# Modulation rows by a table per slot, low halves one tile later, output's first tiles in two parts, context three steps later

## The chip, the cores and the metric

One core of a Trainium2 chip runs one program. The metric is the device time of one execution in microseconds (us). Engines are called PE (matmuls), PEld (weight loads, beside PE), DVE, ACT, POOL and SP (which issues most DMAs).

## The reference, cut to what matters

x is 512 positions by 1024 features. Two blocks run one after the other.

```
first_block, for l in 0, 1:
  mod = (silu(c) @ ada_w[l] + ada_b[l])            # 9 vectors of 1024
  h += 0.5 * mod[0,2] * swiglu(modulated norm of h, ffn_w_in[l,0], ffn_w_out[l,0])
  z = (modulated norm of h) @ mix_w_in[l]          # q, kv, gates, uv, za, zb
  y_a = sparse attention (compressed keys, all blocks, window), 8 heads of 64
  u, v = split(gelu(z_uv)); y_b = u * (causal W_s @ layernorm(v) + b)   # gated unit
  merged = sigmoid(za) * (y_a @ proj_a) + sigmoid(zb) * (y_b @ proj_b)
  h += mod[1,2] * (merged @ w_out[l])
  h += 0.5 * mod[2,2] * swiglu(modulated norm of h, ffn_w_in[l,1], ffn_w_out[l,1])
x = rmsnorm(h)
second_block: pool mixer and squared-relu MLP on latents (512) and context (256), then
  attention over both and a last MLP, modulated by w_ada_2 (for c_2, and partly for c_ctx_2)
```

## The kernel before, in words

**Products.** Every float32 operand of a large product is split into a high half (rounded, type fp32r) and a low half (the remainder), and a product is three matmuls: high x high, high x low, low x high (lines 584 to 586). For weights ACT writes the high half WH (L476) and DVE the low half WL (L489) of each tile of up to 128x2048; for activations likewise (names in H and L, as hH/hL, mH/mL, ybH/ybL, nHc/nLc).

**Slots.** `plan()` lists the 308 weight tiles, called slots, in the order in which PE uses them. There are 2 raw buffers and 4 of WH and WL (NR, NW = 2, 4). Each engine's program is written out by hand and walks the slots: `step_act`, `step_dve` and `step_pool` stand where PE begins slot k; they split the weights of slot k+3, whose buffers are free once slot k-1 is done. SP loads `raw(k+5)` at its turn k, after waiting for the low half of slot k+3.

**Modulation rows.** The vectors mod are computed on DVE: 240 "rows", each a 128x1024 tile of modulation weights times the broadcast condition, summed along the tile (`rows_dve`, L550). `rows_after(k)` says how many rows are done by slot k: one per slot, with pauses. Rows 0 to 143 and 208 to 239 take one such instruction. Rows 144 to 207 serve two conditions and take two 128x512 instructions (L559), a small sum (L563) and the one of L550. Rows from 15 on go through two buffers `araw`. SP's turn k loads, behind `raw(k+5)`, the rows up to one beyond `rows_after(k)`: so of the rows of slot k the first has been loaded a turn earlier, and a second one is issued at turn k, after DVE has done the low half of slot k+3. At slot 128 (`CHANGE`) SP replaces the condition, behind row 143. The steps at entries of a stage (`enter_dve`) do one row more.

**The mixer.** A stage is entered in halves of 256 positions: `both_halves_pe` runs the last product of the stage before (`network_end_pe` or `output_end_pe`, 8 output tiles for each half), while DVE updates h (L1196) and makes the norm. Then `attention1_pe` begins with two slots of key and value columns; ACT copies the first results to `cm`, DVE builds the blocks R from them (L1595, L1599), PE multiplies them (L1378). The attention itself has no slots. After it `gmlp_pe` computes u and v, four tiles "sv" (L1771) in two free PSUM banks, since four are set aside, and DVE makes of each tile: sum with the bias (L1821, which frees the bank), product with u (L1826), wait for ACT's high half (L1793), low half (L1828). `merged_act` and `merged_dve` apply the sigmoids through one scratch tile `scr[0]`. The output product (`output_end_pe`) takes each of 8 tiles through all 8 feature tiles mH/mL in turn; tiles 6 and 7 come last from the merge.

**The last gated network and the context.** In the network of layer 1 that follows the mixer (slots 159 to 195) the second block's context runs beside it: `weave(main, side, pace)` does one step of the network, then `pace(n)` steps of the context, on all four engines alike. `beside_network(n)` is 0 for n = 0, then 1, and 2 where n % 3 == 1. The context's steps: 1 to 3 sums of squares (DVE L661), 4 the sum on PE (L619, its root on ACT, L646), 5 its spread over partitions (L626, which needs DVE's L672), pool slots (w_pool_2) at steps 12, 17, 22 and 27, each needing low halves (L2052) that DVE makes a step earlier, a second norm with the sum at step 31 and the spread at 32, a third at 39 and 40. POOL_CONTEXT places the pool slots in `plan()`. The slots of the context's MLP (196 to 231) have no rows.

Of the kernel before, what the change touches and what calls it, by code (L numbers as in the profile page):

```python
# [6 lines left out]
F32 = mybir.dt.float32  # L7
# [8 lines left out]
S = 512  # L16
# [10 lines left out]
POOL_CONTEXT = (11, 15, 18, 22)  # L27
# [70 lines left out]
CHANGE = 8 * 18 - 16  # L98
# [242 lines left out]
def build(nc, A, out):  # L341
# [3 lines left out]
    with ctx:  # L345
# [159 lines left out]

        def rows_after(k):

            idle = max(0, min(k, SHARED[1] - 1) - SHARED[0] + 1)
            late = min(2, max(0, k - CHANGE + 1))
            return min(8 * len(adas), 17 + k - idle - late)  # L510
# [718 lines left out]
        def output_end_pe(g):  # L1229

            k0 = now.pe
            now.pe += 4

            def group(pe, x, o):
                k, c = k0 + o // 2, lat.half[x].cols
                b, free = take(g, "O", x, o)
                pe.wait_ge(*a_whi.to(k))
                pe.wait_ge(*wlo(k))
                products(pe, k, o % 2, KT, b[:, 0:S // 2], lambda i: (M.mH[:, i, c], M.mL[:, i, c]),
                         lambda i: (a_hhi.to(g, "m", i), v_hlo.to(g, "m", i)), (g, "O", x, o), free)  # L1240
                if x and o % 2:
                    mm.again("slot", k)
            return group
# [13 lines left out]
        def enter_act(act, l, j):  # L1257
            prev, g = stage_before(l, j), f"mix{l}" if j == 1 else f"ffn{l}{j // 2}"
            k0 = now.act
            now.act += 4 if j == 2 else 3  # L1260
            split_act(act, k0 + NW)
            rows_act(act, rows_after(k0) + 1)
            both_halves_act(act, g, mod(1, l, 3 * j), lambda x, i: v_h.to(prev, "O", x, i),
                            output_ahead(k0) if j == 2 else network_ahead(k0))

        def enter_dve(dve, l, j):
# [4 lines left out]
            rows_dve(dve, rows_after(k0) + 1)  # L1271
# [523 lines left out]
        def gmlp_dve(dve, g, l):  # L1795
# [22 lines left out]
            for f in range(4):  # L1818
                v = M.vf[:, f, :].rearrange("p (a b) -> p a b", a=4)
                dve.wait_ge(*mm.to(g, "sv", f))  # L1820
                dve.q.tensor_tensor(v, bank(g, "sv", f)[:, :].rearrange("p (a b) -> p a b", a=4),  # L1821
                                    M.bsb[:, f, :].unsqueeze(1).broadcast_to([128, 4, 128]), ALU.add
                                    ).then_inc(*empties(v_ev, g, "sv", f))
                dve.wait_ge(*v_ev.to(g, "sv", f))
                dve.wait_ge(*a_ev.to(g, "uv", f))
                dve.q.tensor_tensor(M.vf[:, f, :], M.vf[:, f, :], M.uu[:, f, :], ALU.mult).then_inc(*v_ev.up(g, "uv", f))  # L1826
                dve.wait_ge(*a_yhi.to(g, "yb", f))
                dve.q.tensor_tensor(M.ybL[:, f, :], M.vf[:, f, :], M.ybH[:, f, :].bitcast(F32), ALU.subtract  # L1828
                                    ).then_inc(*v_ylo.up(g, "yb", f))
# [14 lines left out]
        def merged_act(act, g):  # L1844
            sg = lat.scr[0]
            before = None
            for m in range(4):
                for which in range(2):
# [3 lines left out]
                    for f in (2 * m, 2 * m + 1):  # L1852
                        act.wait_ge(*mm.to(g, "z", which, f))
                        if before is not None:
                            act.wait_ge(*v_mg.to(*before))
                        act.q.activation(sg[:, :], bank(g, "z", which, f)[:, :], ACT.Sigmoid
                                         ).then_inc(*empties(a_fn, g, "z", which, f))
                        before = (g, "sum", f) if which else (g, "p", 0, f)
# [5 lines left out]
        def merged_dve(dve, g):  # L1864
            sg = lat.scr[0]
            for m in range(4):
                for which in range(2):
# [3 lines left out]
                    for f in (2 * m, 2 * m + 1):  # L1871
                        y = lat.scr[1 + f % 2]
# [691 lines left out]
        def beside_network(n):  # L2564
            return 0 if n < 1 else 1 + (n % 3 == 1)
# [66 lines left out]
        def sp_program(sp):  # L2632
# [33 lines left out]
            loaded = 16  # L2666
            for k in range(len(slots)):
                if k == CHANGE:
# [136 lines left out]
```

## Time and profile before

| what | value |
|---|---|
| median of 3 runs | 3920.36 us (3917.42 to 3921.22) |
| the profiled execution's own time | 3915.16 us |
| its span | 3913.4 us |
| mean granted clock of PE, as a share | 0.962 |
| PE busy | 3668.9 us (94%) |
| DVE, ACT, POOL busy | 2231.8, 1311.4, 341.8 us |

The span runs from the first to the last instruction of the program; the remaining 1.8 us lie around it. In the timeline, the brackets behind an instruction give how long its engine was idle before it and who ended that. In the listing of stretches the granted clock is a share of full speed, 0.50 being the lower of the two levels.

### The profile page before, as it was taken

How to read it: one execution, taken by the hardware profiler on the slowest of the kernel's cores; microseconds unless marked ns; L12 is line 12 of the kernel's file. 1: busy time of each engine (PE TensorE's matmuls, PEld its weight loads, DVE VectorE, ACT ScalarE, POOL GpSimd, SP SyncE). 2: the span in 40 equal slices, each digit the busy share in tenths (PEclk: the TensorE clock that was granted, in tenths of full speed). 3: DMA queues.
4: the chain of work that ended last, by engine and by line, in shares of the span. 5: the costliest groups of instructions: out<-in, count | busy, mean ns of one | idle time of the engine just before them, and what ended most of it. 6: DMA issues, size and time to landing. Idle time of an engine off the chain costs nothing.

```text
span 3913.4 us, 45537 instructions
## 1 busy us (share of the span) xinstructions
PE 3668.9 (94%) x18026; PEld 2962.2 (76%) x18026; DVE 2231.8 (57%) x3607; ACT 1311.4 (34%) x1906; POOL 341.8 (9%) x380
## 2 busy tenths in 40 slices
PE   6999899999999999999999999887799969999997
PEld 5888856788889888855788878777588846577886
DVE  5554644656446545554666767776755555634444
ACT  3222443233223222444224323344322234533221
POOL 0000122000001000112001010134100010200000
PEclk9999999999999999989999999998899968999998
DMA  5433301334432433310343434333233311012221
GB/s 225 167 145 145 120 33 59 127 137 164 146 145 102 183 139 144 126 69 25 124 162 124 149 143 161 124 119 140 87 145 145 135 49 54 1 44 85 89 97 42
DMA packets 84228, 451.93 MB, mean 115 GB/s; under 512 B 10193, under 2 KB 10641, under 8 KB 47153
## 3 DMA queue, kind: packets, MB, share of 16 engines
q1 hardware_dynamic: 81936, 439.35, 30.5%
q0 software_dynamic: 2080, 9.67, 0.7%
q8 instruction: 144, 2.36, 0.2%
q14 instruction: 68, 0.55, 0.0%
HBM read 446.88 MB, written 2.10 MB: 115 GB/s over the span
## 4 chain that ended last, share of the span: by engine, by line
PE 80%; DVE 9%; issue 4%; ACT 4%; DMA 1%; POOL 1%; SPq 0%; DVEq 0%; POOLq 0%; ACTq 0%
PE ps L584 21%; PE ps L586 21%; PE ps L585 21%; PE ps L1453 3%; PE ps L1489 2%; ACT WH L476 1%; DVE WL L489 1%; DVE scrc L1115 1%; PE ps L2418 1%; PE ps L1471 1%; DMA araw<-in_ast 1%; DVE scr L661 1%; PE ps L2392 1%; PE ps L958 1%; PE ps L604 1%
## 5 line engine op out<-in xcount | busy, mean ns | idle before, releaser
L584 PE MATMUL ps<-nH,WH 128*128 128x512 f32 x2416 | 956.9, 396 | 9.2 <-DVE nL L716 7.1
L489 DVE TENSOR_TENSOR WL<-raw,WH 128x2048 fp32r<-128x2048 f32 (+2 forms) x290 | 639.2, 2208 | 555.8 <-ACT WH L476 554.7
L586 PE MATMUL ps<-nH,WL 128*128 128x512 f32 x2416 | 953.1, 395 | 0.0
L585 PE MATMUL ps<-nL,WH 128*128 128x512 f32 x2416 | 951.0, 394 | 0.0
L476 ACT ACTIVATE WH<-raw 128x2048 fp32r<-128x2048 f32 (+2 forms) x308 | 560.0, 1823 | 583.8 <-PE ps L586 554.4
L584 PEld LDWEIGHTS ps<-nH,WH 128*128 128x128 f32 x2416 | 457.7, 189 | 118.7 <-issue 10.4
L585 PEld LDWEIGHTS ps<-nL,WH 128*128 128x128 f32 x2416 | 457.6, 189 | 103.5 <-issue 2.2
L586 PEld LDWEIGHTS ps<-nH,WL 128*128 128x128 f32 x2416 | 457.3, 189 | 99.4
L584 PE MATMUL ps<-hH,WH 128*128 128x512 f32 x1072 | 422.2, 394 | 2.2 <-DVE h L1185 2.2
L586 PE MATMUL ps<-hH,WL 128*128 128x512 f32 x1072 | 421.8, 393 | 0.0
L585 PE MATMUL ps<-hL,WH 128*128 128x512 f32 x1072 | 421.5, 393 | 0.0
L550 DVE SCALAR_TENSOR_TENSOR araw<-araw,cB 128x1024 f32<-128x1024 f32 x225 | 276.5, 1229 | 73.3 <-DMA araw<-in_ast 73.2
L1068 ACT ACTIVATE hH<-scr 128x512 fp32r<-128x512 f32 x152 | 96.1, 632 | 456.7 <-DVE scr L1112 382.9
L584 PEld LDWEIGHTS ps<-hH,WH 128*128 128x128 f32 x1072 | 201.4, 188 | 48.5 <-DVE h L1185 2.7
L585 PEld LDWEIGHTS ps<-hL,WH 128*128 128x128 f32 x1072 | 201.4, 188 | 46.2
L586 PEld LDWEIGHTS ps<-hH,WL 128*128 128x128 f32 x1072 | 201.4, 188 | 46.2
L1061 ACT ACTIVATE scr<-ps 128x512 f32<-128x512 f32 x152 | 89.5, 595 | 387.5 <-PE ps L586 379.2
L931 POOL TENSOR_SCALAR scr<-scr,der,mods 128x256 f32<-128x256 f32 x80 | 61.8, 773 | 1532.9 <-DVE scr L844 1532.0
L1118 DVE TENSOR_TENSOR hL<-scr,hH 128x512 fp32r<-128x512 f32 x152 | 105.3, 692 | 106.1 <-ACT hH L1068 106.1
L1185 DVE SCALAR_TENSOR_TENSOR h<-ps,der,h 128x512 f32<-128x512 f32 x144 | 102.6, 747 | 66.9 <-PE ps L586 65.4
L2108 DVE TENSOR_TENSOR ma<-ma,ps 128x512 f32<-128x512 f32 x112 | 74.7, 684 | 111.6 <-PE ps L586 111.2
L1664 DVE TENSOR_REDUCE st<-ps 128x1 f32<-128x128 f32 (+3 forms) x128 | 62.0, 486 | 111.1 <-PE ps L1455 111.0
(357 smaller groups left out, 5432.6 us busy)
## 6 DMA issues: line engine op xcount, KB each, us to landing
raw<-in_wst SPq DMA_DIRECT2D x282, 1024.0 KB, 4.8
araw<-in_ast SPq DMA_DIRECT2D x225, 512.0 KB, 5.7
raw<-in_wst SPq DMA_DIRECT2D x18, 512.0 KB, 3.6
row<-in_ast SPq DMA_DIRECT2D x15, 512.0 KB, 15.0
cw<-in_cw POOLq DMA_DIRECT2D x4, 1024.0 KB, 6.0
h<-in_xT SPq DMA_DIRECT2D x1, 2048.0 KB, 8.3
raw<-in_wst SPq DMA_DIRECT2D x8, 256.0 KB, 2.6
out<-h SPq DMA_DIRECT2D x8, 256.0 KB, 2.0
```

The lines of the kernel that those rows point to most:

```text
L476: act.q.activation(M.WH[k % NW][:, 0:n], M.raw[k % NR][:, 0:n], ACT.Copy).then_inc(*a_whi.up(k))
L489: dve.q.tensor_tensor(M.WL[k % NW][:, 0:n], M.raw[k % NR][:, 0:n], M.WH[k % NW][:, 0:n].bitcast(F32), ALU.subtract).then_inc(*v_wlo.up(k))
L550: dve.q.scalar_tensor_tensor(out=w[:, :], in0=w[:, :], scalar=1.0, in1=M.cB[q][:, :], op0=ALU.mult, op1=ALU.mult, accum_out=total).then_in ...
L584: pe.q.matmul(to, hi[:, i, cc], xh, start=i == 0, stop=False)
L585: pe.q.matmul(to, hi[:, i, cc], xl, start=False, stop=False)
L586: t = pe.q.matmul(to, lo[:, i, cc], xh, start=False, stop=i == nk - 1)
L1061: act.q.activation(p.scr[n % 2][:, 0:N], bank(g, "a", ci, f)[:, 0:N], ACT.Silu if gated else ACT.Relu).then_inc(*empties(a_fn, g, "a", ci, f))
L1068: act.q.activation(hH[:, ci % 2, f, :], p.scr[2 + f % 2][:, 0:N], ACT.Copy).then_inc(*a_hhi.up(g, ci, f))
L1118: dve.q.tensor_tensor(hL[:, ci % 2, f, :], p.scr[2 + u][:, 0:N], hH[:, ci % 2, f, :].bitcast(F32), ALU.subtract).then_inc(*v_hlo.up(g, ci, f))
L1185: dve.q.scalar_tensor_tensor(out=M.h[:, o, :], in0=bank(g, "o", ci, o)[:, :], scalar=gate[:, o:o + 1], in1=M.h[:, o, :], op0=ALU.mult, op1 ...
L1453: pe.q.matmul(b[:, 0:nk], M.q[half, hh // 2, 128 * qt:128 * qt + 128], K[half, 0:nk], start=True, stop=False, skip_group_check=True)
L1489: t = pe.q.matmul(to[half, 128 * x:512], M.Vt[br - 1][:, x, 64 * grp:64 * grp + 64], M.PT[br - 1][:, x, 128 * x:512], start=br == 1 and x ...
```

## The change

It has five parts.

1. `row_steps` makes a table `row_plan`: 1 row per slot, 2 at every third slot (k % 3 == 0) whose array's name begins with f (the gated networks), 0 at the last three output slots of each gated network but the last, at the mixer's first six slots, at proj_a, proj_b and w_out, and at the slots 196 to 231 as before. The row extra at entries is gone. The swap of the condition comes at slot 123 where the table holds still at 144 for two slots.
2. `gmlp_dve`: the low half of a tile comes after the sum and product of the next tile.
3. `merged_act`, `merged_dve`: two scratch tiles (scr[0], scr[3]) for the sigmoids in turn.
4. `output_end_pe`: the first four tiles of the first half are taken through feature tiles 0 to 5, and then all four through 6 and 7.
5. `beside_network(n)` is 0 for n < 4, then 1, and 2 where n is even; POOL_CONTEXT moves by one or two slots.

```diff
-POOL_CONTEXT = (11, 15, 18, 22)
+POOL_CONTEXT = (13, 16, 20, 23)
...
-CHANGE = 8 * 18 - 16
+def row_steps(slots, total):
+    done, out, waited = 16, [], 0
+    for k, (a, idx, r0, nk, c0, n) in enumerate(slots):
+        more = 2 if k % 3 == 0 and a[0] == "f" else 1
+        if a == "ffn_w_out" and r0 >= 16 * 128 and idx != (1, 1):
+            more = 0
+        if a == "mix_w_in" and c0 <= 1280 or a in ("proj_a", "proj_b", "w_out"):
+            more = 0
+        if SHARED[0] <= k < SHARED[1]:
+            more = 0
+        if done == 8 * 18 and waited < 2:
+            more, waited = 0, waited + 1
+        elif done < 8 * 18:
+            more = min(more, 8 * 18 - done)
+        done = min(total, done + more)
+        out.append(done)
+    return out
...
+                if x == 0 and o < 4:
+                    if o == 0:
+                        four(pe)
+                    return
...
+            def four(pe):
+                c, to = lat.half[0].cols, []
+                for o in range(4):
+                    b, free = take(g, "O", 0, o)
...
+                for part in (range(6), range(6, 8)):
+                    for o in range(4):
...
+                        for i in part:
+                            pe.wait_ge(*a_hhi.to(g, "m", i))
+                            pe.wait_ge(*v_hlo.to(g, "m", i))
...
-            rows_dve(dve, rows_after(k0) + 1)
+            rows_dve(dve, rows_after(k0))
...
-            for f in range(4):
+            for f in range(5):
+                if f < 4:
...
+                if f:
+                    dve.wait_ge(*a_yhi.to(g, "yb", f - 1))
...
         def beside_network(n):
-            return 0 if n < 1 else 1 + (n % 3 == 1)
+            return 0 if n < 4 else 1 + (n % 2 == 0)
...
-                if k == CHANGE:
+                if loaded == 8 * 18 + 1 and k and row_plan[k - 1] == 8 * 18 and not changed:
+                    changed = True
                     sp.wait_ge(*v_row.to(8 * 18 - 1))
```

What the table moves, in numbers of rows done: at slot 29 it stands at 56 in place of 46, at slot 62 at 68 in place of 79, at 158 at 157 in place of 173, at 195 at 207 in place of 210, and both end at 240, at slot 264 in place of 261. From slot 159 to 195 it has 50 rows, 13 of the 37 slots taking two; before, counting those of the wide first step from 171 on, 39 rows were done there.

**First place: DVE at the start of the first layer's mixer.** WL is a weight's low half, araw a row, R the blocks that PE waits for. Before:

```order
L489 TENSOR_TENSOR WL0_11<-raw0_5,WH0_7 128x2048
L550 SCALAR_TENSOR_TENSOR araw0_15,mods_20<-araw0_15,cB0_17 128x1024
L550 SCALAR_TENSOR_TENSOR araw1_16,mods_20<-araw1_16,cB0_17 128x1024
L550 SCALAR_TENSOR_TENSOR araw0_15,mods_20<-araw0_15,cB0_17 128x1024
L1595 COPY R_71<-cm0_69 64x16x31 x4
L1599 TENSOR_TENSOR R_71<-R_71,pe_73 128x992
```

After (its line numbers are those of the changed kernel):

```order
L869 TENSOR_TENSOR nL_4<-scr3_28,nH_3 128x256
L510 TENSOR_TENSOR WL3_14<-raw1_6,WH3_10 128x2048
L510 TENSOR_TENSOR WL0_11<-raw0_5,WH0_7 128x2048
L1643 COPY R_71<-cm0_69 64x16x31 x4
L1647 TENSOR_TENSOR R_71<-R_71,pe_73 128x992
```

Three rows have left the place between the weights' low halves and R.

**Second place: PE around the context's first sum and spread.** nH/nL are the network's input, scrc the context's scratch. Before, the sum and the spread stand apart:

```order
L586 MATMUL ps0<-nH_3,WL3_14 128x512
L619 MATMUL ps2<-ones_23,scrc2_101 128x1 x2
L584 MATMUL ps1<-nH_3,WH0_7 128x512
...
L586 MATMUL ps3<-nH_3,WL0_11 128x512
L626 MATMUL ps4<-scrc3_102,ones_23 128x256
L584 MATMUL ps5<-nH_3,WH1_8 128x512
```

After:

```order
L606 MATMUL ps0<-nH_3,WL2_13 128x512
L639 MATMUL ps2<-ones_23,scrc2_101 128x1 x2
L646 MATMUL ps1<-scrc3_102,ones_23 128x256
L604 MATMUL ps3<-hH_54,WH3_10 128x512
```

The 48 matmuls of a slot that stood between them are gone, and the pair has moved 144 matmuls back.

**Third place: DVE at the last slot of that network.** h is updated from the banks that PE wants back, nLc is the context's low half. Before:

```order
L1185 SCALAR_TENSOR_TENSOR h_1<-ps2,der_21,h_1 128x512
L725 TENSOR_TENSOR scrc0_99<-xc_97,ps4 128x256
L716 TENSOR_TENSOR nLc_105<-scrc2_101,nHc_98 128x256
L725 TENSOR_TENSOR scrc1_100<-xc_97,ps4 128x256
L716 TENSOR_TENSOR nLc_105<-scrc3_102,nHc_98 128x256
L489 TENSOR_TENSOR WL2_13<-raw0_5,WH2_9 128x2048
L550 SCALAR_TENSOR_TENSOR araw1_16,mods_20<-araw1_16,cB0_17 128x1024
L1185 SCALAR_TENSOR_TENSOR h_1<-ps1,der_21,h_1 128x512
```

After:

```order
L736 TENSOR_TENSOR nLc_105<-scrc3_102,nHc_98 128x256
L510 TENSOR_TENSOR WL2_13<-raw0_5,WH2_9 128x2048
L579 SCALAR_TENSOR_TENSOR ps6,half_34<-araw1_16,cB0_17 128x512
L579 SCALAR_TENSOR_TENSOR ps7,half_34<-araw1_16,cB0_17 128x512
L583 TENSOR_TENSOR mods_20<-half_34 128x1
L570 SCALAR_TENSOR_TENSOR araw1_16,mods_20<-araw1_16,cB1_18 128x1024
L579 SCALAR_TENSOR_TENSOR ps6,half_34<-araw0_15,cB0_17 128x512
L579 SCALAR_TENSOR_TENSOR ps7,half_34<-araw0_15,cB0_17 128x512
L583 TENSOR_TENSOR mods_20<-half_34 128x1
```

One simple row has become two of the later kind, and four low halves of the context stand ahead of them in place of two.

## Rows read from the trace of the kernel before

**Rows 1.** The page: span, and busy time, share and instructions of each engine.
```profile
span 3913.4 us, 45537 instructions
...
PE 3668.9 (94%) x18026; PEld 2962.2 (76%) x18026; DVE 2231.8 (57%) x3607; ACT 1311.4 (34%) x1906; POOL 341.8 (9%) x380
```

**Rows 2.** Waits of PE: who waited <- for whom: us in total, times, longest.
```profile
PE ps L1378 <- DVE R L1599: 13.6, 2, 9.3
...
PE ps L619 <- DVE scrc L661: 8.9, 1, 8.9
...
PE ps L1771 <- DVE vf L1821: 7.5, 3, 4.0
...
PE ps L584 <- DVE mL L1886: 7.1, 4, 2.4
```

**Rows 3.** Timeline of DVE, both mixers' starts: start, us, instruction, [idle before].
```profile
432.82 4.49 DVE L489 TENSOR_TENSOR WL<-raw,WH 128x2048 fp32r<-128x2048 f32 x2 [1.12 <-ACT WH L476]
...
445.13 2.33 DVE L1595 COPY R<-cm 64x496 f32<-64x496 f32 x4
...
1641.89 2.33 DVE L1595 COPY R<-cm 64x496 f32<-64x496 f32 x4
```

**Rows 4.** Timeline of ACT at the same two places.
```profile
438.52 1.08 ACT L1498 ACTIVATE cm<-ps 128x512 f32<-128x512 f32 x2 [3.99 <-PE ps L960]
...
1640.24 1.09 ACT L1498 ACTIVATE cm<-ps 128x512 f32<-128x512 f32 x2 [1.46 <-PE ps L960]
```

**Rows 5.** Timeline of PE, three waits.
```profile
716.84 0.47 PE L584 MATMUL ps<-nH,WH 128*128 128x512 f32 x1 [1.23 <-DVE vf L1821]
...
2303.35 0.36 PE L584 MATMUL ps<-nHc,WH 128*128 128x256 f32 x1 [3.67 <-DVE nHc L2052]
...
2472.38 0.51 PE L584 MATMUL ps<-hH,WH 128*128 128x512 f32 x1 [2.22 <-DVE h L1185]
```

**Rows 6.** Timeline of DVE, gated unit of the first layer.
```profile
705.63 2.29 DVE L489 TENSOR_TENSOR WL<-raw,WH 128x2048 fp32r<-128x2048 f32 x1
709.31 1.23 DVE L550 SCALAR_TENSOR_TENSOR araw<-araw,cB 128x1024 f32<-128x1024 f32 x1 [1.38 <-DMA araw<-in_ast]
...
710.57 0.69 DVE L1821 TENSOR_TENSOR vf<-ps,bsb 128x512 f32<-128x512 f32 x1
```

**Rows 7.** Timeline of DVE, two rows of the later kind.
```profile
2044.18 0.69 DVE L559 SCALAR_TENSOR_TENSOR ps<-araw,cB 128x512 f32<-128x512 f32 x1
...
2050.80 0.70 DVE L559 SCALAR_TENSOR_TENSOR ps<-araw,cB 128x512 f32<-128x512 f32 x1 [3.88 <-DMA araw<-in_ast]
```

**Rows 8.** Stretches: us, busy (instructions), granted clock, DMA share, GB/s.
```profile
706.00:720.00 14.00, 9.21 (x80) 1.00 0.49 180
...
840.00:844.00 4.00, 4.00 (x23) 0.57 0.19 33
...
2038.00:2045.00 7.00, 5.04 (x22) 0.52 0.02 7
...
2303.00:2308.00 5.00, 4.65 (x18) 0.66 0.02 4
```

**Rows 9.** The stretch of the last gated network, all engines.
```profile
2100.00:2486.00 386.00, 367.95 (x1671) 303.86 (x1669) 280.71 (x512) 128.51 (x155) 21.45 (x30) 0.98 0.41 150
```

**Rows 10.** Timeline of DVE, last slot of that network.
```profile
2468.11 2.29 DVE L489 TENSOR_TENSOR WL<-raw,WH 128x2048 fp32r<-128x2048 f32 x1 [1.36 <-ACT WH L476]
2470.32 1.22 DVE L550 SCALAR_TENSOR_TENSOR araw<-araw,cB 128x1024 f32<-128x1024 f32 x1
...
2471.58 4.70 DVE L1185 SCALAR_TENSOR_TENSOR h<-ps,der,h 128x512 f32<-128x512 f32 x7
```

**Rows 11.** Timeline of ACT, root of the context's first sum.
```profile
2153.70 1.28 ACT L646 ACT_TABLE_LOAD   x1
2154.99 0.26 ACT L646 ACTIVATE rsc<-ps,epsc 128x2 f32<-128x2 f32 x1
```

More of the change, by code:

```diff
@@ L502, in split_pool @@
                                      ALU.subtract).then_inc(*p_wlo.up(k))
+        row_plan = row_steps(slots, 8 * len(adas))
         def rows_after(k):
-            idle = max(0, min(k, SHARED[1] - 1) - SHARED[0] + 1)
-            late = min(2, max(0, k - CHANGE + 1))
-            return min(8 * len(adas), 17 + k - idle - late)
+            return row_plan[k]
         def row_tile(j):
@@ L1817, in gmlp_dve @@
             dve.wait_ge(*ld_bsb.to(l))
-            for f in range(4):
[L1819 to L1829, printed above, removed]
+            for f in range(5):
+                if f < 4:
+                    v = M.vf[:, f, :].rearrange("p (a b) -> p a b", a=4)
+                    dve.wait_ge(*mm.to(g, "sv", f))
+                    dve.q.tensor_tensor(v, bank(g, "sv", f)[:, :].rearrange("p (a b) -> p a b", a=4),
+                                        M.bsb[:, f, :].unsqueeze(1).broadcast_to([128, 4, 128]), ALU.add
+                                        ).then_inc(*empties(v_ev, g, "sv", f))
+                    dve.wait_ge(*v_ev.to(g, "sv", f))
+                    dve.wait_ge(*a_ev.to(g, "uv", f))
+                    dve.q.tensor_tensor(M.vf[:, f, :], M.vf[:, f, :], M.uu[:, f, :], ALU.mult).then_inc(*v_ev.up(g, "uv", f))
+                if f:
+                    dve.wait_ge(*a_yhi.to(g, "yb", f - 1))
+                    dve.q.tensor_tensor(M.ybL[:, f - 1, :], M.vf[:, f - 1, :], M.ybH[:, f - 1, :].bitcast(F32), ALU.subtract
+                                        ).then_inc(*v_ylo.up(g, "yb", f - 1))
         def gmlp_pool(pool, g, l):
@@ L1844, in merged_act @@
         def merged_act(act, g):
-            sg = lat.scr[0]
-            before = None
+            before = [(), ()]
             for m in range(4):
@@ L1852, in merged_act @@
                     for f in (2 * m, 2 * m + 1):
+                        sg = lat.scr[3 * (f % 2)]
                         act.wait_ge(*mm.to(g, "z", which, f))
-                        if before is not None:
-                            act.wait_ge(*v_mg.to(*before))
+                        if before[f % 2]:
+                            act.wait_ge(*v_mg.to(*before[f % 2]))
                         act.q.activation(sg[:, :], bank(g, "z", which, f)[:, :], ACT.Sigmoid
                                          ).then_inc(*empties(a_fn, g, "z", which, f))
-                        before = (g, "sum", f) if which else (g, "p", 0, f)
+                        before[f % 2] = (g, "sum", f) if which else (g, "p", 0, f)
                         if which:
@@ L1864, in merged_dve @@
         def merged_dve(dve, g):
-            sg = lat.scr[0]
             for m in range(4):
```

19 lines of the change are left out of this document (16 added, 3 removed).

## The prediction

> **What bounds the kernel now.** I read the page first: in a span of 3913.4 us PE is busy for 3668.9, DVE for 2231.8 and no other engine for half of it [rows 1]. So the kernel is PE's, and a change that takes no matmul away can only win from PE's idle time (about 240 us) and from stretches at the lower clock. Then the waits of PE, grouped by who ended them: the reader is to see that the first product of the mixer (L1378) waits 13.6 us in two waits for R, the sum of squares of the context 8.9 us in one, the gated unit (L1771) 7.5 us in three, and the output product (L584) 7.1 us in four for mL [rows 2]. Those four are the targets. All end at DVE, so the next views are DVE's timelines at these places and the order of DVE's work. The profiled execution took 3915.16 us; the median of the three runs is 5.2 us more. The sum is made against the former, and the 5.2 is added at the end. A difference of 0.2%, 7.8 us, is about what a measurement of this kernel tells from none.
>
> **Rows out of the mixer's start (part 1).** In the first layer the first copy cm is ready half way into ACT's 1.08 us, at 439.1 [rows 4]; DVE has finished the weights' low halves at 437.3, but stands in three rows until 445.13, where R begins [rows 3]. The rows leave this place. R can begin at 439.1: minus 6.0 us on PE's wait of 9.3, which is long enough to take it. In the second layer cm is ready at 1640.8 and R begins at 1641.89: minus 1.1. The rows themselves go to later slots, which I cost below. **-7.1.**
>
> **Gated unit (parts 1, 2).** In the first layer DVE waits 1.38 us for a row's transfer and takes 1.26 for the row, and then comes the first sum, at 710.57 [rows 6]. Without the row that sum starts at 707.9. From there on a tile now takes 2.7 us (sum, product, a wait for ACT, low half); with the low half one tile later the wait goes: 1.4 us to the second sum and 2.1 to the third, which so ends at 712.1. PE's next stage waits for exactly this third sum and began at 716.84 [rows 5]; it begins at 712.2, minus 4.7. In the second layer the row is one of the later kind: two halves, a small sum and a full one, 0.69 + 0.69 + 0.1 + 1.26, or 2.74 us [rows 6, 7], without a wait for its transfer, and I get minus 4.9. **-9.6.** The 7.5 us of L1771 [rows 2] and a part of the 1.23 behind them bound this from above; from below it is nothing, if the sigmoids that follow then wait for PE.
>
> **Output in two parts (part 4).** Tile 0 reaches feature tile 6 after 18 matmuls of 256 columns now, and after 72 then. One takes 4.00 us / 23 at a clock of 0.57 [rows 8], so some 0.1 us at full clock: 54 more are 5 us of cover or more, and no single wait for mL is longer than 2.4. All four waits, 7.1 us [rows 2], go. Behind each pair PE ran slow: 4.0 us at 0.57 and 7.0 us at 0.52 [rows 8]. Against full clock that is 4.0 x 0.43 = 1.7 and, of 5.04 us busy, 0.48 x 5.04 = 2.4. Without a wait the clock has no reason to fall: minus 4.1. The four tiles end close together, so their banks come free later, but four other banks are there for tiles 4 to 7. **-11.2.**
>
> **Two scratch tiles (part 3).** DVE's sigmoid chain gets shorter in a stretch where PE does not wait for it once the output's cover is there. Nothing; without the cover it would be worth at most one of the mL waits, 2.4 us.
>
> **Context three steps later (part 5, with the table).** Here something is gained and more is lost.
> Gained: at step 4 the squares have long been summed when PE comes, three network slots later, and the wait of 8.9 us goes [rows 2]; so does the one of 3.67 for nHc at the second pool slot's place [rows 5], where a dependent pair now falls elsewhere. **-12.6.**
> Lost, first: with two steps at every even n, three dependent pairs run back to back, without a slot of 48 matmuls in between: steps 4 and 5 (sum, then spread), 16 and 17 (low halves, then the pool slot that reads them), 31 and 32 (sum, spread). Before, one pair did, steps 21 and 22, and that is the wait of 3.67. A chain sum, root, reciprocal, spread is at least the root of 0.26 and the table load of 1.28 before it [rows 11] and at most the 8.9 of rows 2. I take 3.67, the row of the same kind of pair, for all three: **+11.0** (bounds 4.6 and 27).
> The Trainium skill, "ScalarE: Activation LUTs", section "What ACT_TABLE_LOAD costs", says a switch of tables is the load and then a drain of 1380 ns. In the trace the root starts at 2154.99, right at the load's end (2153.70 + 1.28) [rows 11], so I leave the drain out; by the page the two sum pairs would cost an estimated 2.8 us more and the gain would be so much smaller.
> Lost, second, at the last slot: between the weights' low half and the updates of h, for which PE waits (2.22 us), DVE has one simple row, 2470.32 to 2471.58 [rows 5, 10]. Now there are two rows of the later kind, 5.5 us, and the second one's transfer is issued only in this turn: I price its wait by the 3.88 in front of such a row [rows 7]. 9.4 in place of 1.3: **+8.1** (bounds 4.2, with no transfer wait, and 8.1 plus one low half of 2.29). The two low halves of nLc that stand ahead are work moved, not added.
> Lost, third, the clock: the new waits put PE to the lower level about twice, as in the two stretches above: **+4.1** (bounds nothing and 8).
> DVE in this stretch: 280.7 us busy in 386 [rows 9], 11 more rows of 2.74 make 311, and 13 double slots with 3.88 of waiting make 361. PE needs 368. I take it that DVE, which works three slots ahead, just keeps up. **+10.6 in all.**
> On the clock row and rule part. The gated unit's stretch has 4.8 us of idle in 14 and a clock of 1.00; the one behind the wait of 3.67 has 0.66 [rows 8]. The Trainium skill, "TensorE: Matmul & The Clock Gate", section "HAM oscillation — how this bites in real kernels", tells of waits between tiles that put PE back to the cold clock time after time. By it all three pairs would be followed by such a stretch, about 2 us more than I count; the gated unit's stretch speaks against that for short waits, the other for it.
>
> **Other slots.** Two rows at every third slot of the other gated networks add 1.3 us and a transfer's wait, on a DVE that is busy for 57% [rows 1] and runs three slots ahead: nothing. If that cover were gone, some 28 slots at 1.3 us or more would be on the path.
>
> **Sum.** -7.1 - 9.6 - 11.2 + 10.6 = -17.3, so 3897.9 for the profiled execution and 3903 for the median.
>
> **The rivals.**
> 1. *The network's stretch hides its new work.* The pairs find their input ready, because DVE and ACT do in time what PE asks for, and no clock is lost: the context costs -12.6 + 8.1 = -4.5, the sum is -32.4, 3888 us. For it: DVE has 105 us idle there [rows 9]. Against: back to back means that the second step's input does not exist when PE arrives. Chance 0.18.
> 2. *Half the double slots show.* A slot is 386 / 37 = 10.4 us. DVE's share in a double one is 2.3 + 5.5 + 3.9 = 11.7 and the network's own work. If each of the 13 gives PE 1 us of waiting, the sum is -4, 3916 us. Chance 0.17.
> 3. *DVE becomes the bound (slower).* To the 361 us come DVE's waits for ACT's high halves, 1.36 us before the last one [rows 10]; 37 of them are 50. If rows' transfers and these waits never overlap, the stretch takes 411 us, 25 more than now, and with the last slot's 8.1, the pairs' 11.0 and the clock the context costs about +44: +16 in all, 3936 us. From a loss of 36 us in slots 159 to 195 on, the kernel is measurably slower (28 gained elsewhere, and 7.8). Chance 0.08.
> 4. *The early parts do not arrive.* R comes 6 us earlier, but the attention behind it is a chain in which PE waits for DVE and ACT anyway, so the time is waited for later, and so behind the gated unit with the sigmoids. Without those two parts half or all is lost: -17.3 + 12 gives about 3915. For it: a released PE often meets the next wait. Against: the attention's DVE work does not grow. Chance 0.12.
>
> My forecast has 0.45, and its own range is 3895 to 3910. The range of 8 in 10 goes from 3886 (rival 1) to 3917 (rivals 2 and 4). Faster by over 0.2% is below 3912.5: the forecast, rival 1 and some of the others, 0.75. Within 0.2%: 0.16. Slower: 0.09, rival 3 and its edges.
>
> **What would show it.** Right: R's first copy near 439 and L1378's waits down to about 6.5 us in all; one DVE wait fewer in each gated unit; no wait for mL at the output; the sum of the context without its 8.9; new PE waits of 2 to 5 us at three pairs, and one of about 10 before the last slot's next stage, behind two rows of L579. Wrong: PE waiting for WL in slots 159 to 195 (rival 3), no new waits there at all (rival 1), or attention as much longer as R came earlier (rival 4).

## The result and the profile after

The change makes the kernel slower: 3957.03 us median (3949.79 to 3960.1, 4 runs) against 3919.32 us, a ratio of 1.0094 (95% interval 1.0076 to 1.0111). Forecast were 3903 us, and faster. Of all runs reported here one is left out as slow, at 4789.14 us and a mean granted clock of 0.712 (24 rows, in the second table of the experiments). The profiled execution took 3955.57 us, 40.4 more than that of before.

The page of the changed kernel, the lines that answer to [rows 1]:

```profile
span 3953.8 us, 45557 instructions
...
PE 3681.6 (93%) x18026; PEld 2971.2 (75%) x18026; DVE 2231.2 (56%) x3607; ACT 1310.1 (33%) x1906; POOL 340.8 (9%) x380
```

PE has 12.7 us more of busy time for the same 18026 instructions, and 28 us more of idle time. Where it happens is read from the same instructions on PE's timeline, before and after (starts, where no end is named; us from the start of the span):

| instruction on PE | before | after | difference |
|---|---|---|---|
| first product with R, layer 0 | 448.83 | 443.80 | -5.0 |
| first product behind the gated unit, layer 0 | 716.84 | 704.23 | -12.6 |
| first product with R, layer 1 | 1645.59 | 1629.53 | -16.1 |
| first product of the output, layer 1 | 2033.59 | 2013.90 | -19.7 |
| end of that output | 2085.1 | 2058.5 | -26.6 |
| first sum behind the last gated network | 2505.49 | 2544.47 | +39.0 |
| end of the last product of the kernel | 3899.7 | 3940.1 | +40.4 |

So the mixers gain 26.6 us, close to the 28 that were forecast, and from the end of that output to the first sum behind the network, the last gated network with the context beside it, 65.6 us are lost: 486.0 us in place of 420.4. This is "the stretch" below.

**The mixers.** DVE's timeline, where R is built in layer 0 and in layer 1 (answers to [rows 3]):

```profile
440.08 2.35 DVE L1643 COPY R<-cm 64x496 f32<-64x496 f32 x4 [1.68 <-ACT cm L1546]
...
1625.82 2.35 DVE L1643 COPY R<-cm 64x496 f32<-64x496 f32 x4 [1.84 <-ACT cm L1546]
```

R's copy now waits for ACT's cm and for nothing else. The gated unit on DVE, layer 0 (answers to [rows 6]):

```profile
700.14 0.69 DVE L1870 TENSOR_TENSOR vf<-ps,bsb 128x512 f32<-128x512 f32 x1
...
701.48 0.68 DVE L1870 TENSOR_TENSOR vf<-ps,bsb 128x512 f32<-128x512 f32 x1
...
...
703.40 0.68 DVE L1870 TENSOR_TENSOR vf<-ps,bsb 128x512 f32<-128x512 f32 x1
```

From the first sum to the second it is 1.34 us, to the third 1.92 more (1.4 and 2.1 in the forecast), and no wait for ACT stands between. PE's timeline at the three places (answers to [rows 5]), the third being the start of the output in layer 0:

```profile
443.80 0.41 PE L1426 MATMUL ps<-R,cw 128*128 128x62 f32 x2 [3.33 <-DVE R L1647]
...
704.23 0.47 PE L604 MATMUL ps<-nH,WH 128*128 128x512 f32 x1 [0.44 <-DVE vf L1870]
...
822.16 0.36 PE L1284 MATMUL ps<-mH,WH 128*128 128x256 f32 x1 [1.64 <-DVE mL L1935]
```

PE waits 3.33 us for R in place of 9.3, and 0.44 us behind the gated unit in place of 1.23. The third wait is new. Before, PE went into the output without a wait and waited at feature tiles 6 and 7; now it waits 1.64 us before the very first product.

**The stretch.** PE's waits in it: who waited, for whom, us in total, times, longest.

```profile
PE ps L604 <- DVE h L1205: 25.4, 4, 13.0
PE ps L646 <- DVE scrc L692: 19.8, 2, 10.0
PE ps L639 <- DVE scrc L681: 17.1, 3, 10.6
PE ps L604 <- DVE nHc L2101: 5.4, 2, 3.0
```

They are 68 us; in the kernel before, the sum waited 8.9, nHc 3.7 and h 2.2 us [rows 2, 5], and the spread (L646 now) not at all. No wait of PE there is for a weight's low half WL. DVE's own waits in the stretch, before:

```profile
DVE WL L489 <- ACT WH L476: 44.9, 28, 4.3
...
DVE ps L559 <- DMA araw<-in_ast: 11.7, 6, 3.9
```

and after:

```profile
DVE ps L579 <- DMA araw<-in_ast: 57.6, 21, 4.8
DVE WL L510 <- ACT WH L497: 31.5, 22, 2.8
```

The waits for a row's transfer have grown from 11.7 to 57.6 us. The listing of the stretch, all engines, before and after (columns as in [rows 9]):

```profile
2085.10:2505.40 420.30, 395.36 (x1898) 330.83 (x1896) 303.87 (x558) 147.96 (x188) 29.92 (x41) 0.98 0.40 147
```

```profile
2058.50:2544.40 485.90, 409.89 (x1898) 340.51 (x1896) 336.81 (x647) 147.17 (x188) 27.68 (x41) 0.92 0.37 139
```

The same 1898 instructions of PE take 409.9 us in place of 395.4, at a clock of 0.92 in place of 0.98. So 14.5 of the 65.6 us are the lower clock, and 51 are PE's idle time. DVE is busy for 33 us more.

### The profile page after: what moved, and what is told of

It reads as the page before. It is cut to its first block, busy times and chain, and to the rows that moved or that the text cites. A ratio compares the mean times of both kernels' runs of the same rounds, so it can differ in the third digit from the quotient of the medians.

```text
span 3953.8 us, 45557 instructions
## 1 busy us (share of the span) xinstructions
PE 3681.6 (93%) x18026; PEld 2971.2 (75%) x18026; DVE 2231.2 (56%) x3607; ACT 1310.1 (33%) x1906; POOL 340.8 (9%) x380
## 4 chain that ended last, share of the span: by engine, by line
PE 76%; DVE 10%; issue 5%; ACT 5%; DMA 3%; POOL 1%; DVEq 0%; SPq 0%; POOLq 0%; ACTq 0%
PE ps L604 19%; PE ps L605 19%; PE ps L606 19%; PE ps L1501 3%; DMA araw<-in_ast 2%; PE ps L1537 2%; ACT WH L497 2%; DVE WL L510 2%; DVE scrc L1135 1%; PE ps L2467 1%; PE ps L1519 1%; DVE ps L579 1%; PE ps L1238 1%; PE ps L978 1%; PE ps L1240 1%
## 5 line engine op out<-in xcount | busy, mean ns | idle before, releaser
L604 PE MATMUL ps<-hH,WH 128*128 128x512 f32 x1072 | 429.1, 400 | 25.4 <-DVE h L1205 25.4
L1088 ACT ACTIVATE hH<-scr 128x512 fp32r<-128x512 f32 x152 | 96.0, 632 | 520.2 <-DVE scr L1132 445.7
L606 PEld LDWEIGHTS ps<-hH,WL 128*128 128x128 f32 x1072 | 204.3, 191 | 48.2
L579 DVE SCALAR_TENSOR_TENSOR ps<-araw,cB 128x512 f32<-128x512 f32 x128 | 88.2, 730 | 57.6 <-DMA araw<-in_ast 57.6
```

The lines of the kernel that those rows point to most:

```text
L579: dve.q.scalar_tensor_tensor(out=banks[6 + x][:, :], in0=w[:, cut], scalar=1.0, in1=M.cB[q][:, cut], op0=ALU.mult, op1=ALU.mult, accum_out ...
L604: pe.q.matmul(to, hi[:, i, cc], xh, start=i == 0, stop=False)
L606: t = pe.q.matmul(to, lo[:, i, cc], xh, start=False, stop=i == nk - 1)
L1088: act.q.activation(hH[:, ci % 2, f, :], p.scr[2 + f % 2][:, 0:N], ACT.Copy).then_inc(*a_hhi.up(g, ci, f))
```

## The experiments

All medians are of the runs of that kernel; ratios are to the kernel before on the same chip. "Theory R" is that the table of rows makes DVE late in the stretch, "theory P" that the context's pace does.

### Rows and pace, taken apart

Old pace:

```diff
-POOL_CONTEXT = (13, 16, 20, 23)
+POOL_CONTEXT = (11, 15, 18, 22)
-            return 0 if n < 4 else 1 + (n % 2 == 0)
+            return 0 if n < 1 else 1 + (n % 3 == 1)
```

> The changed kernel with the old pace and the old places of the pool slots; the table of rows stays. Theory R (the table: 50 later-kind rows, 13 double slots, each second row loaded only in its turn, hold up DVE in slots 159 to 195, where the trace of the change shows 66 us lost): most of the loss stays, 3935 to 3955 us. Theory P (the pace: dependent pairs of steps back to back expose the chain through ACT and DVE): most of the loss goes, 3895 to 3910 us.

Old rows:

```diff
-            return row_plan[k]
+            idle = max(0, min(k, SHARED[1] - 1) - SHARED[0] + 1)
+            late = min(2, max(0, k - 128 + 1))
+            return min(8 * len(adas), 17 + k - idle - late)
...
-            rows_dve(dve, rows_after(k0))
+            rows_dve(dve, rows_after(k0) + 1)
```

> The changed kernel with the old formula for the rows (also the row extra at entries and the old place of the swap); the new pace stays. Theory R: slots 159 to 195 lose no more than 10 us against the kernel before, and with the output in two parts and the low halves one tile later (about 16 us gained without the rows' part) it is at 3905 to 3915 us. Theory P: the stretch still loses 40 us or more, 3940 to 3955 us.

Both:

> The changed kernel with old rows and old pace, so only the low halves one tile later, the two scratch tiles and the output in two parts stand. Both theories: faster than before by the output's 11 us and 3 to 7 us of the gated unit, 3901 to 3908 us; R wait in the mixer as before (13.6 us). Above 3915 would say that the output in two parts gains less than the shifts of the changed kernel suggest.

And only the order of SP's loads in the changed kernel:

```diff
+                while loaded < min(rows_after(k), 8 * len(adas)):
+                    row(loaded)
+                    loaded += 1
                 if k + NR + NW - 1 < len(slots):
                     raw(k + NR + NW - 1)
                 while loaded < min(rows_after(k) + NA - 1, 8 * len(adas)):
```

> The changed kernel, but SP issues the rows of a turn's own slot ahead of that turn's weights, so a double slot's second row is under way about a slot earlier. 13 waits of 3.5 us for a row's transfer, some 45 us of DVE's time in slots 159 to 195, go. If it is these waits that hold DVE up (theory R in the form of transfers): 3905 to 3925 us. If it is the instructions of the 11 added rows (30 us) or the pace: 3940 us or more.

Measured, with the length of the stretch in each profiled run, read as above:

| rows | pace | slot's own rows | stretch, us | median, us | ratio (interval) |
|---|---|---|---|---|---|
| old | old | as before (parts 2 to 4 alone) | 421.9 | 3914.31 | 0.9992 (0.9983 to 1.0002) |
| old | new | as before | 431.6 | 3927.92 | 1.0027 (1.0016 to 1.0039) |
| new | old | as before | 474.0 | 3937.99 | 1.0053 (1.0038 to 1.0068) |
| new | new | as before (the change) | 486.0 | 3957.03 | 1.0094 (1.0076 to 1.0111) |
| new | new | first | 452.1 | 3913.74 | 0.9990 (0.9978 to 1.0001) |

In the stretch the two add: the table costs 52 us at the old pace and 54 at the new, the pace 10 with the old rows and 12 with the new. Both theories hold, with 4 or 5 parts to one for R. Theory R's time came with the old pace (3937.99 in 3935 to 3955) and not with the old rows (3927.92 where 3905 to 3915 was expected); of theory P neither came (3895 to 3910, and 3940 to 3955). With the old rows and the new pace PE waits so in the stretch:

```profile
PE ps L648 <- DVE scrc L694: 15.6, 2, 9.5
...
PE ps L606 <- DVE nHc L2103: 3.2, 1, 3.2
```

The sum waits no more, as forecast for the new pace, and the three dependent pairs wait 18.8 us in all, where the forecast had 11.0. The last run of the table says what it is in the rows: the same 50 rows, the same instructions on DVE, and 34 us of the stretch and 43 us of the median are back (41 by the two ratios), from two loads changing places in SP's queue. Of the us outside the stretch, 6 are PE's clock in the attention of layer 0, which differs from profile to profile (last section). DVE's waits in the stretch of that run:

```profile
DVE ps L579 <- DMA araw<-in_ast: 14.2, 9, 4.0
```

43 us of waiting for transfers are gone (57.6 to 14.2). What is left of PE's waits there is mostly the pace's and the last slot's:

```profile
PE ps L646 <- DVE scrc L692: 20.5, 2, 10.2
PE ps L604 <- DVE h L1205: 13.9, 3, 10.4
```

The run with old rows and old pace held a surprise too: 3914.31 where 3901 to 3908 was expected. There PE waits before the first product it can start in the output, 2.93 us in layer 0:

```profile
837.59 0.36 PE L1286 MATMUL ps<-mH,WH 128*128 128x256 f32 x1 [2.93 <-DVE mL L1937]
```

and 4.41 in layer 1, where rows stand ahead of the merge. The output in two parts lost at its start most of what it gained at its end: its end stands 2.0 us earlier in layer 0 relative to the projections before it, and 0.8 us later in layer 1. The low halves one tile later, alone, gave 2.0 and 1.5 us.

### Pairs, and fewer rows in the stretch

A pace that never puts a dependent pair back to back:

```diff
-POOL_CONTEXT = (13, 16, 20, 23)
+POOL_CONTEXT = (13, 16, 19, 22)
-            return 0 if n < 4 else 1 + (n % 2 == 0)
+            return 0 if n < 4 else 1 + (n in (4, 7, 8, 10, 12, 13, 15, 16, 18, 19, 21, 22) if n < 26 else n % 3 == 1)
```

> The changed kernel with another pace: the context still begins at n = 4 and takes two steps where it can, but never a sum and its spread, or low halves and the pool slot that reads them, one behind the other without a slot of the network between. Theory P2 (the two spreads, 9.8 and 10.0 us of PE's waiting in the changed kernel, are exposed only by the pairs): 3930 to 3942 us. Rival (DVE is late by its rows, and whoever stands next waits): 3950 to 3960 us, with the waits under other names.

It gave 3957.9 us (1.0096, 1.0064 to 1.0128) and a stretch of 487.3. The rival had it. The spread's two waits of 10 us are gone, and others have grown (in the changed kernel h had 25.4 and the sum 17.1):

```profile
PE ps L604 <- DVE h L1205: 38.9, 8, 10.9
PE ps L639 <- DVE scrc L681: 26.4, 3, 12.6
```

Then with the slot's own rows first and rows moved out of the stretch:

```diff
-        more = 2 if k % 3 == 0 and a[0] == "f" else 1
+        last = idx == (1, 1) and a[0] == "f"
+        more = 2 if k % 3 == 0 and a[0] == "f" and (not last or k == 165) else 1
...
-        if a == "mix_w_in" and c0 <= 1280 or a in ("proj_a", "proj_b", "w_out"):
+        if a == "mix_w_in" and c0 <= 1280 or idx != (1,) and a in ("proj_a", "proj_b", "w_out"):
```

> SP issues the slot's own rows first, the context runs at the old pace, and the table gives one row to each slot of proj_a, proj_b and w_out of the second layer and single rows (one double) to slots 159 to 195, so 38 rows there in place of 50. Theory R (rows and transfers): the mixers' gain stays (27 us, or 37 as in the run with the second row first) and the stretch loses nothing: 3880 to 3895 us. If the rows in the merge cost there what they cost in the network: 3900 to 3910 us.

> The run before it with the pace without pairs in place of the old one. The first sum's wait (8.8 us in the kernel before) and the pool slot's (3.7) go and nothing comes: 8 to 13 us below the run before it, 3870 to 3885 us. If the later start only crowds the context's DVE work into fewer slots: the same as the run before it or slower.

And with rows taken earlier still (w_out's slots take a row too, in both layers). Like all edits of this part, it stands against the changed kernel:

```diff
-        more = 2 if k % 3 == 0 and a[0] == "f" else 1
+        more = 2 if k % 2 == 0 and a[0] == "f" and idx != (1, 1) else 0 if k > 181 and idx == (1, 1) else 1
...
-        if a == "mix_w_in" and c0 <= 1280 or a in ("proj_a", "proj_b", "w_out"):
+        if a == "mix_w_in" and c0 <= 1280 or idx != (1,) and a in ("proj_a", "proj_b"):
```

> As the run before it, but rows taken far earlier (two at every second slot of the first three gated networks) so that slots 159 to 195 have 24 rows and none behind slot 181. If DVE's load in that stretch, or the row ahead of the last update of h (2.2 us of waiting before), still costs: 3 to 8 us below the run before it. If the added rows in networks without the context cost as much as they save: equal. If double rows at every second slot make DVE late there: up to 20 us above.

| rows in slots 159 to 195 | pace | stretch, us | median, us | ratio (interval) |
|---|---|---|---|---|
| 38 | old | 428.8 | 3899.85 | 0.9949 (0.9931 to 0.9966) |
| 38 | no pairs | 431.3 | 3899.02 | 0.9952 (0.9933 to 0.9971) |
| 24 | no pairs | 417.7 | 3894.46 | 0.9936 (0.9918 to 0.9953) |

The pace without pairs, which I expected to be worth 8 to 13 us once DVE was in time, is worth nothing at 38 rows: a miss. With the old pace and 38 rows the time, 3899.85, fell between the two expectations (3880 to 3895, or 3900 to 3910). The third run's stretch is the first that is shorter than before, by 3 us, but that is no more than two profiles with this part unchanged differ by (420.4, and 423.2 in the kernel before with only the loads' order changed, below); and the intervals of the second and third run overlap, so a gain of one on the other is not shown.

### The bank wait, the order of loads, and what adds up

```diff
                 if x == 0 and o < 4:
-                    if o == 0:
-                        four(pe)
+                    if o % 2 == 0:
+                        four(pe, o)
                     return
...
-                for o in range(4):
+                for o in (o0, o0 + 1):
                     b, free = take(g, "O", 0, o)
```

> The changed kernel, but the first half's first four output tiles are taken two and two: tiles 0 and 1 through feature tiles 0 to 5 and then 6 and 7, and so 2 and 3. In the changed kernel PE waits 1.64 us in each layer before the very first product of the output. If that wait is for banks (four at once, the last of them freed by the sigmoid of tile 7), it goes: two are free, and 36 products (4 us) still cover mL 6 and 7. Locally 3 us less, 3951 to 3957 us in all. If the wait is for mL itself, it only moves behind the first part and the time stays.

Measured: 3945.98 us (1.0067, 1.0053 to 1.0081), 11 us under the change and more than I gave it. PE's timeline at the start of the output of layer 1, the last product of proj_b and the first of the output:

```profile
2000.38 0.39 PE L606 MATMUL ps<-ybH,WL 128*128 128x512 f32 x1
2000.62 0.28 PE L1284 MATMUL ps<-mH,WH 128*128 128x256 f32 x1
```

No wait stands there, nor in layer 0, nor behind the first part for mL. From the last projection to the end of the output PE gains 4.9 us in layer 0 and 6.7 in layer 1 against the kernel before, where the changed kernel gained 1.8 and 5.1. That is 4.7 us locally, of which 3.6 are the two waits; the rest lies within the 1.5 us by which the four tiles' output differs between profiles with the same code (46.1 us in the change, 44.6 in the run with the slot's own rows first, layer 0). What the run gained beyond that is not explained by the edit: in the attention of layer 1 its profile gains 9.4 us on the changed kernel's with the same code, by PE's clock (last section). So the wait was for banks: with two tiles it went, and none for mL took its place. That the last of the four is freed by ACT's sigmoid of tile 7 fits the changed kernel's timeline of ACT (it ends at 821.85, PE starts at 822.16), but was not tried by itself:

```profile
821.27 0.58 ACT L1906 ACTIVATE scr<-ps 128x512 f32<-128x512 f32 x1
```

> The changed kernel with the slot's own rows issued first and the context at the old pace: 50 rows stand in slots 159 to 195, their transfers are ahead. If the costs add as they did between the four runs with old and new rows and pace (pace 11 us): 3900 to 3908 us, and the stretch some 20 us longer than before, by the instructions of the 11 rows alone. If the pace only costs when DVE is late by its transfers: 3912 to 3918 us, as with the new pace.

Measured: 3895.75 us (0.9944, 0.993 to 0.9957), stretch 434.5. It is under the expected 3900, and the pace is worth 18 us here, more than the 10 and 12 of the first table. PE's waits in its stretch:

```profile
PE ps L604 <- DVE h L1205: 12.0, 4, 7.3
PE ps L639 <- DVE scrc L681: 9.7, 1, 9.7
```

> The kernel before with only the order of SP's loads changed (the slot's own rows first). It has no double slots, so a slot's row is already loaded a turn earlier in either order: 3912 to 3922 us, no difference. A gain of 10 us or more would say that the runs with this order owe it to something else than the double slots.

Measured: 3918.76 us, 0.9999 (0.999 to 1.0008). The order of the loads does nothing where no slot has two rows.

The version put together from all of it, of which the edit of the table is shown:

```diff
-        more = 2 if k % 3 == 0 and a[0] == "f" else 1
+        more = 2 if k % 2 == 0 and a[0] == "f" and idx != (1, 1) else 0 if k > 184 and idx == (1, 1) else 1
...
-        if a == "mix_w_in" and c0 <= 1280 or a in ("proj_a", "proj_b", "w_out"):
+        if a == "mix_w_in" and c0 <= 1280 or idx != (1,) and a in ("proj_a", "proj_b") or k in (140, 153, 154):
```

> The version put together from what the runs showed: slot's own rows first; two rows at every second slot of the first three gated networks, 26 rows in slots 159 to 195 and none behind 184; no row ahead of the gated unit's tiles and of the last merge tiles in the second layer; the pace without pairs; the output two tiles at a time. Against the run with early rows (3895.8 us) the waits of 4.3 us (gated unit) and 4.4 us (output) in the second layer go: 3884 to 3892 us. If DVE's rows in the earlier networks or the clock there give it back: 3893 to 3900 us.

Measured: 3884.62 us over 5 runs (3870.44 to 3890.27), a ratio of 0.9915 (0.9902 to 0.9929): it beats the kernel before by 35 us and the change by 72. Its profiled run is the fastest of the five, 14 us under the median. PE's waits for the sum and for h in its stretch, and the stretch's listing:

```profile
PE ps L639 <- DVE scrc L681: 5.6, 2, 3.5
PE ps L604 <- DVE h L1205: 5.0, 4, 2.5
...
2038.80:2461.40 422.60, 400.25 (x1899) 333.71 (x1897) 277.62 (x487) 145.64 (x186) 30.00 (x41) 0.98 0.36 132
```

DVE is busy for 277.6 us there, 26 less than before, and the clock is at 0.98 again. The stretch takes 422.6 us, 2 more than before: it gains nothing, but it lets through the 46 us that this profile is ahead at its start (2038.8 against 2085.1). Of these 46, 19 lie in the two attentions, where PE's clock is higher than in the profile of the kernel before (7.7 and 11.3 us from the first product with R to the start of the gated unit). No edit aimed at that, and how much of the median's 35 us it is, is open.

## Why the prediction was wrong

**The rows out of the mixer's start: right.** PE's waits for R shrank by 6.0 and 1.0 us, forecast 6.0 and 1.1. In layer 0 the product came only 5.0 us earlier, since 0.9 us had been lost ahead of it. The rows were the wait.

**The gated unit: right.** -4.8 in layer 0, where I had -4.7, and -5.0 in layer 1, where I had -4.9. Between R and the gated unit of layer 0 another 2.8 us fell to PE's clock in the attention, which I had not counted.

**The output in two parts: the mechanism right, the banks overlooked.** Forecast were -5.6 a layer, measured -1.8 and -5.1. The failing sentence is "their banks come free later, but four other banks are there for tiles 4 to 7". It looked at the banks behind the four tiles and not at those in front: four must be free at once when the first product starts, and they are not. Two tiles at a time gave -4.9 and -6.7, 11.6 us in all, where 11.2 was forecast.

That the mixers together gained 26.6 us, so near the 28 forecast, is in part luck: the output fell 4.3 us short, and PE's clock in the attention of layer 0 (2.8 us) and small pieces made up for it.

**The context and the table in the stretch: wrong, +65.6 for +10.6.** The failing step is "I take it that DVE, which works three slots ahead, just keeps up". The budget put 361 us of DVE beside 368 of PE, in a window of 386 us where the stretch has 420, and called it even. The runs take the 65.6 us apart, in this order: back to the old pace 12.0 (486.0 to 474.0), the slot's own rows loaded first 39.5 (474.0 to 434.5), and the rest, 14.1, comes with the 11 more rows and their places. In another order the shares differ by some us: the pace was worth 10 to 18.

Term by term, of the 51 us of idle time 8.2 are the sum (17.1 in place of 8.9, where I had it at nothing), 1.7 the low halves nHc (5.4 for 3.7), 19.8 the two spreads, and 23.2 the updates of h (25.4 for 2.2), of which I had counted the last slot alone; 2.3 are saved at nLc (1.6 for 3.9, each wait 1.0 us at most). So the gain of 12.6 did not come. With the old rows it did: there the sum waits no more, and the new pace costs its pairs. The table took it back. Three things were missing.

First, a transfer's wait in a double slot is not DVE's idle time to be added up and compared with a total. It lies between two rows, behind which everything of that slot stands. DVE's timeline in the changed kernel, from the low half of one slot to that of the next and the network's L1132 behind it:

```profile
2146.39 2.29 DVE L510 TENSOR_TENSOR WL<-raw,WH 128x2048 fp32r<-128x2048 f32 x1 [1.30 <-ACT WH L497]
...
2150.11 1.22 DVE L570 SCALAR_TENSOR_TENSOR araw<-araw,cB 128x1024 f32<-128x1024 f32 x1
...
2154.86 0.70 DVE L579 SCALAR_TENSOR_TENSOR ps<-araw,cB 128x512 f32<-128x512 f32 x1 [3.52 <-DMA araw<-in_ast]
...
2157.64 0.95 DVE L681 TENSOR_TENSOR scrc<-scrc,scrc 128x256 f32<-128x256 f32 x2
2158.51 2.29 DVE L510 TENSOR_TENSOR WL<-raw,WH 128x2048 fp32r<-128x2048 f32 x1
...
2162.42 1.22 DVE L570 SCALAR_TENSOR_TENSOR araw<-araw,cB 128x1024 f32<-128x1024 f32 x1
...
2163.79 0.69 DVE L1132 TENSOR_TENSOR scr<-scr,ps 128x512 f32<-128x512 f32 x1
```

The first row ends at 2151.3, the second waits 3.52 us for its transfer, and the context's last squares (L681), for which PE waits with the sum, come at 2157.64. The chain of waits in the stretch shows the same: by line, and two of the pieces.

```profile
by line: DMA araw<-in_ast 17.3%; issue 12.5%; DVE WL L510 9.3%; PE ps L604 9.2%; PE ps L606 8.8%; PE ps L605 8.8%; DVE ps L579 6.7%; ACT WH L497 6.2%; DVE araw L570 2.8%; DVE scr L1132 2.7%; ACT hH L1088 1.9%; DVE h L1205 1.7%; ACT scrc L66
...
2128.24 5.61 DMA araw<-in_ast
...
2149.12 5.64 DMA araw<-in_ast
```

The transfer starts 0.44 us after the end of the low half WL (2146.39 + 2.29, then 2149.12), since the weights' load, which waits for that low half, stands ahead of it in SP's queue. At 17.3% of the chain, no other line has a larger share. I had priced this wait rightly (3.88 us, 13 times) and put it on the wrong side: as something that fills DVE's slack. There is no slack for PE to draw on when PE waits not for the weights, which are three slots ahead, but for h, for the squares and for what the spread reads, which are made in the slot in which they are needed.

Second, the price of a pair. I took 3.67 us for each. The sum–spread pair costs 9.84 and 9.96. PE's timeline and ACT's at the first:

```profile
2158.74 0.98 PE L639 MATMUL ps<-ones,scrc 128*128 128x1 f32 x4 [10.62 <-DVE scrc L681]
2169.56 0.77 PE L646 MATMUL ps<-scrc,ones 128*128 128x256 f32 x1 [9.84 <-DVE scrc L692]
```

```profile
2164.51 0.63 ACT L1088 ACTIVATE hH<-scr 128x512 fp32r<-128x512 f32 x1 [13.43 <-DVE scr L1132]
...
2167.14 1.28 ACT L666 ACT_TABLE_LOAD   x1
2168.44 0.26 ACT L666 ACTIVATE rsc<-ps,epsc 128x2 f32<-128x2 f32 x1
```

The sum starts at 2158.74, the root only at 2168.44. In between ACT makes hH (L1088) for the network's next product, and that waits for DVE's L1132, which stands behind a low half and a row (2158.51 to 2163.79 above). With the old rows the three pairs wait 9.5, 3.2 and 6.1: 3.67 was right for the low halves and the pool slot that reads them, and too little for a sum and its spread. In the changed kernel PE would have waited for what stands there anyway: without pairs the time stayed (3957.9). With the slot's own rows first the spreads still wait 20.5 us, and the old pace gives 18 us back. Whether there the pairs or the late start cost them is open: the pace without pairs was not run at 50 rows with the transfers ahead, and at 38 rows it equals the old pace.
The Trainium skill, "ScalarE: Activation LUTs", section "What ACT_TABLE_LOAD costs", puts a drain behind the load; here the root starts 0.02 us after the load's end (2167.14 + 1.28), so the trace of the change again shows none.

Third, the clock. I had +4.1, it is 14.5. The Trainium skill, "TensorE: Matmul & The Clock Gate", section "HAM oscillation — how this bites in real kernels", says that waits for transfers between tiles throw PE back again and again. I had weighed it as about 2 us more than I counted. The trace agrees with its direction: 68 us of waits in pieces of up to 13 brought the stretch from 0.98 to 0.92, and the version put together, whose waits for the sum and for h are 10.6 us, is back at 0.98.

**The last slot: DVE's delay right, PE's wait longer.** DVE and PE at that slot:

```profile
2500.04 2.29 DVE L510 TENSOR_TENSOR WL<-raw,WH 128x2048 fp32r<-128x2048 f32 x1 [1.36 <-ACT WH L497]
2502.25 0.69 DVE L579 SCALAR_TENSOR_TENSOR ps<-araw,cB 128x512 f32<-128x512 f32 x1
...
2508.53 0.70 DVE L579 SCALAR_TENSOR_TENSOR ps<-araw,cB 128x512 f32<-128x512 f32 x1 [3.54 <-DMA araw<-in_ast]
...
2511.31 3.38 DVE L1205 SCALAR_TENSOR_TENSOR h<-ps,der,h 128x512 f32<-128x512 f32 x5
```

```profile
2512.11 0.79 PE L604 MATMUL ps<-hH,WH 128*128 128x512 f32 x1 [13.04 <-DVE h L1205]
```

From the start of the first row to the updates of h it is 9.1 us in place of 1.3, with a transfer's wait of 3.54: +7.8, forecast +8.1. PE's wait grew by 10.8, which is just above the upper bound of 10.4 (8.1 and a low half of 2.29). Where no row stands behind slot 184 it is gone (0.96 us at that place).

**The rivals.** Number 3, DVE as the bound, came nearest and had a chance of 0.08 and a price of +16; the profile lost 40.4. Its number for the stretch, about 44 us, was nearer to 65.6 than the 10.6 of the forecast, but its terms as listed (25, 8.1, 11.0 and 4.1) add up to 48.2, or to 35.6 with the gain of 12.6. Its mechanism is not what the trace shows: DVE is busy for 336.8 of 485.9 us, and the sign named for it, PE waiting for WL in these slots, stands nowhere. Its time was near by luck. DVE is not the bound as a total; it is late with single results. Rival 4 fell: what R and the gated unit gained reached the end of the mixers.

## What to carry to other kernels

When work is moved into a slot, ask what stands behind it on its engine and is due in that same slot; being three slots ahead with the weights says nothing about a residual update, a sum or a spread. Count an added load where its queue lets it start, and look first whether the load may go ahead of the one beside it: here that alone gave back 34 us of the stretch. A product that opens several accumulators at once needs all their banks at its start; four tiles waited 1.6 us or more for them, and two at a time did not wait.

## What the runs showed of the hardware

A row's transfer of 512 KB takes 5.6 us (5.61 and 5.64 in the two pieces of the chain), and with the 0.44 before it the first row of 2.7 us hides less than half of it.

The attention is not equally fast from profile to profile with the same code, and the difference is PE's clock. In layer 1, from the first product with R to the start of the gated unit, PE does the same 1130 matmuls in the changed kernel (first two lines) and in the one with two tiles (last two); the second line of each is the 16 us in which they part (columns as in [rows 9]):

```profile
1629.50:1888.80 259.30, 257.41 (x1130) 165.28 (x1130) 127.35 (x318) 104.11 (x235) 47.46 (x74) 0.94 0.14 51
1685.50:1701.50 16.00, 16.00 (x43) 7.62 (x43) 6.55 (x24) 6.51 (x22) 4.84 (x8) 0.50 0.11 46
```

```profile
1627.40:1877.30 249.90, 248.00 (x1130) 161.38 (x1130) 126.95 (x318) 104.20 (x235) 47.69 (x74) 0.98 0.15 53
1683.40:1699.40 16.00, 16.00 (x75) 8.01 (x75) 9.58 (x35) 9.28 (x31) 6.83 (x12) 1.00 0.10 42
```

In the 5 us ahead of it (1680 to 1685, and 1677.9 to 1682.9) PE is busy for 4.1 us in both, with the same instructions and one wait, of 0.92 and 0.93 us; one clock then fell to the lower level and the other did not. What decides it is open. In the profiles of this case this length of attention takes 248 to 260 us, near 250 in eight of the twenty times with the table of rows and in none of the eight with the rows as before. That is more than most edits here are worth, so the edits were read locally and the totals by the medians.
